# Conditioning pieces in runs, sample steps on GpSimd and rotary halves crossed by ScalarE in a hybrid decoder step

## The reference

```
mod = (silu(c) @ w_ada[l] + b_ada[l]).reshape(B, 9, D)        # conditioning, 1 prompt row + 8 sample rows
hh  = rmsnorm(x, g_pre) * (1 + m_scale) + m_shift             # before every sub-layer, per sequence
x   = x + 0.5 * m_gate * rmsnorm(f, g_post)                   # after it
proj = hh @ w_in_even                                         # layer 1: q k qi ki v wi | rq rk (4 heads) rv rg
rope(x): cat(x1*cos - x2*sin, x2*cos + x1*sin)                # rq, rk: halves of 64 of each head's 128 columns
```

## Time and profile before

| | |
|---|---|
| runs | 1423.23 us median of 3 (1422.56 to 1423.35) |
| profiled execution | 1422.14 us; its span on the core 1420.5 us |
| granted TensorE clock, mean over the span | 0.990 of full speed |
| busy in the span | PE 1357.0 us (96%), DVE 789.7 (56%), ACT 613.5 (43%), POOL 87.5 (6%) |
| pieces from POOL's queue | 96 loads of 512 KB, 4.8 us to landing (median) |

### The profile page before, as it was taken

How to read it: one execution, slowest core, us unless ns; L and a number is a source line. 1 busy time by engine, 2 the same in 40 slices (tenths; PEclk the granted TensorE clock), 3 DMA queues, 4 the chain that set the end, 5 groups by cost and what they waited for, 6 DMA issues and landing times.

```text
span 1420.5 us, 24392 instructions
## 1 busy us (share of the span) xinstructions
PE 1357.0 (96%) x9798; PEld 1256.7 (88%) x9798; DVE 789.7 (56%) x1446; ACT 613.5 (43%) x1043; POOL 87.5 (6%) x139
## 2 busy tenths in 40 slices
PE   5899999999999998999999899999989999999996
PEld 2799999979886697999999799999978888999996
DVE  1544444576697777444445743445567976444444
ACT  2534333444343455334344533334457755333342
POOL 0000000003001101000000100000011100000000
PEclk9799999999999999999999999999999999999998
DMA  9565655456249755564355556444466643444442
GB/s 364 209 210 197 205 178 187 147 199 227 90 160 341 258 210 208 180 205 151 120 163 163 206 179 207 163 135 138 159 242 224 224 163 106 148 148 150 129 150 83
DMA packets 82260, 260.08 MB, mean 183 GB/s; under 512 B 11634, under 2 KB 22962, under 8 KB 82034
## 3 DMA queue, kind: packets, MB, share of 16 engines
q1 hardware_dynamic: 65682, 199.56, 41.9%
q0 software_dynamic: 16480, 59.15, 12.0%
HBM read 254.45 MB, written 4.23 MB: 182 GB/s over the span
## 4 chain that ended last, share of the span: by engine, by line
PE 82%; DVE 10%; DMA 3%; ACT 3%; issue 2%; SPq 1%; DVEq 0%; ACTq 0%
PE ps L1614 25%; PE ps L1615 25%; PE ps L1616 25%; PE ps L1679 3%; DMA lent_lo<-in_ada 1%; DVE w_lo L2077 1%; DVE f L2159 1%; DVE x L2145 1%; DVE f L2165 1%; DVE f L2141 1%; DVE xn_lo L2153 1%; DMA x<-in_x 1%; PE ps L589 1%; DMA a_raw<-in_ada 1%; PE ps L1701 1%
## 5 line engine op out<-in xcount | busy, mean ns | idle before, releaser
L1614 PE MATMUL ps<-xn_hi,w_hi 128*128 128x320 f32 x1808 | 573.6, 317 | 21.6 <-DVE xn_lo L2153 18.2
L1616 PE MATMUL ps<-xn_hi,w_lo 128*128 128x320 f32 x1808 | 560.9, 310 | 0.0
L1615 PE MATMUL ps<-xn_lo,w_hi 128*128 128x320 f32 x1808 | 560.8, 310 | 0.0
L2077 DVE TENSOR_TENSOR w_lo<-w_raw,w_hi 128x1024 fp32r<-128x1024 f32 (+1 forms) x357 | 382.3, 1108 | 128.3 <-ACT w_hi L1884 127.7
L1614 PEld LDWEIGHTS ps<-xn_hi,w_hi 128*128 128x128 f32 x1808 | 341.4, 189 | 50.6 <-issue 29.6
L1884 ACT ACTIVATE w_hi<-w_raw 128x1024 fp32r<-128x1024 f32 x362 | 331.6, 961 | 88.8 <-PE ps L1616 78.3
L1615 PEld LDWEIGHTS ps<-xn_lo,w_hi 128*128 128x128 f32 x1808 | 341.7, 189 | 1.4
L1616 PEld LDWEIGHTS ps<-xn_hi,w_lo 128*128 128x128 f32 x1808 | 341.5, 189 | 0.0
L1614 PE MATMUL ps<-mid_hi,w_hi 128*128 128x320 f32 x704 | 218.3, 310 | 0.3 <-DVE w_lo L2077 0.3
L1616 PE MATMUL ps<-mid_hi,w_lo 128*128 128x320 f32 x704 | 217.3, 309 | 0.0
L1615 PE MATMUL ps<-mid_lo,w_hi 128*128 128x320 f32 x704 | 217.3, 309 | 0.0
(11 more groups left out here) (282 smaller groups left out, 962.1 us busy)
## 6 DMA issues: line engine op xcount, KB each, us to landing
w_raw<-in_gu SPq DMA_DIRECT2D x176, 512.0 KB, 4.5
a_raw<-in_ada POOLq DMA_DIRECT2D x96, 512.0 KB, 4.8
w_raw<-in_down SPq DMA_DIRECT2D x64, 512.0 KB, 3.6
w_raw<-in_pj SPq DMA_DIRECT2D x58, 512.0 KB, 5.1
w_raw<-in_down SPq DMA_DIRECT2D x64, 192.0 KB, 3.6
a_raw<-in_ada SPq DMA_DIRECT2D x16, 512.0 KB, 7.1
w_raw<-in_ada SPq DMA_DIRECT2D x16, 512.0 KB, 6.6
lent_hi<-in_ada SPq DMA_DIRECT2D x8, 512.0 KB, 10.8
```

The costliest lines, as they stand in the source:

```text
L1614: pe.matmul(out, hi, xhi, start=start, stop=False)
L1615: pe.matmul(out, hi, xlo, start=False, stop=False)
L1616: return pe.matmul(out, w_lo[s][:, w_at:w_at + P], xhi, start=False, stop=stop)
L2077: dve.tensor_tensor(w_lo[s][:, cols], w_raw[:, s, cols], w_hi[s][:, cols].bitcast(F32), ALU.subtract).then_inc(w_split, 1)
```

## The change

Four things. (1) `ADA_PLAN`: pieces that were multiplied one at a time between tiles come in runs: gate0 at tiles 3, 7, 11, 15, 19 (4 each; before, one at each of tiles 2 to 21), down0 at block 1 (4; before, one at blocks 0 to 3), gate1 and gate2 at tiles 8 and 13 (4 each; before, one at tiles 6 to 13), odd tail behind blocks 5, 10 and 13 (4, 4, 5; before, one behind each of 4 to 15, two behind 5). Three transposes come one place earlier. (2) At the five boundaries the two sample steps of chunks 2 to 7 go to POOL (`samples`), chunk by chunk, after its loads for the boundary. (3) DVE's order there becomes `late_chunks`, with no pairs. (4) For blocks 10 to 17 PE's permutation is gone: ACT copies each half of the block from PSUM to the other half's partitions of `rope_b`, then the block to `proj`; the sign is in the sin table.

```diff
-ADA_PLAN += [("gate0", c, 1 if c > 1 else 0) for c in range(FC)]
-ADA_PLAN += [("down0", m, 1 if m < 4 else 0) for m in range(KC)]
+ADA_PLAN += [("gate0", c, 4) for c in (3, 7, 11, 15, 19)] + [("down0", 1, 4)]
...
-ADA_PLAN += [("gate1", c, 1 if 6 <= c < 14 else 0) for c in range(FC)]
+ADA_PLAN += [("gate1", c, 4) for c in (8, 13)]
...
-ADA_PLAN += [("gate2", c, 1 if 6 <= c < 14 else 0) for c in range(FC)]
+ADA_PLAN += [("gate2", c, 4) for c in (8, 13)]
...
-ADA_PLAN += [("odd_tail", q, 2 if q == 5 else 1) for q in range(4, 2 * KC)] + [("odd_out", ("first", 2), 3)]
+ADA_PLAN += [("odd_tail", 5, 4), ("odd_tail", 10, 4), ("odd_tail", 13, 5)] + [("odd_out", ("first", 2), 3)]
...
-ADA_TURNS = {("front", 1): [0], ("front", 2): [1], ("gate0", 9): [2], ("gate0", 17): [3], ("down0", 3): [4],
+ADA_TURNS = {("front", 1): [0], ("front", 2): [1], ("gate0", 8): [2], ("gate0", 16): [3], ("down0", 2): [4],
...
             ada_load(gp, pieces[A_SLOTS:KC])
+            for k in range(2, KC):
+                samples(gp, stage, k)
+
+        def samples(gp, stage, k):
+
+            sub = PNORM[stage]
+            fs = tokens(f[:, k, PTOK:TOK])
+            gp.wait_ge(xr_ready, 8 * sub + k + 1)
+            gp.tensor_tensor(fs, fs, per_sample(modT[:, scale_at(sub, k), 1:NCOND]), ALU.mult).then_inc(scaled_s, 1)
+            gp.wait_ge(scaled_s, (KC - 2) * (sub - 1) + k - 1)
+            gp.tensor_tensor(fs, fs, per_sample(modT[:, shift_at(sub, k), 1:NCOND]), ALU.add).then_inc(xmod_ready, 1)
...
                 if b <= 9:
-                    rotate(b - 2, b - 2, 0)
-                elif B_RQK < b <= B_RQK + 8:
-                    rotate(b - 1, b - 1 - (B_RQK - 8), 1)
+                    rotate(b - 2, b - 2)
...
+                    if B_RQK <= b < B_RQK + 8:
+                        act.wait_ge(rope_done, CR + b + h - 3)
+                        for to, of in ((0, HD), (HD, 0)):
+                            last = act.activation(rope_b[to:to + HD, h, :], ps[of:of + HD, 2 * j + h, 0:TOK], kinds[h][0],
+                                                  scale=kinds[h][1])
+                        last.then_inc(crossed, 1)
                     act.activation(proj[:, b + h, :], ps[:, 2 * j + h, 0:TOK], kinds[h][0], scale=kinds[h][1])\
...
+            def rotate_halves(b, par):
+
+                dve.wait_ge(p_evac, PB + b + 1)
+                src = proj[:, b, :]
+                dve.wait_ge(crossed, b - B_RQK + 1)
+                steps.did(dve.tensor_tensor(rope_b[:, par, :], rope_b[:, par, :], ropet[:, 3, :], ALU.mult))
+                steps.did(dve.tensor_tensor(src, src, ropet[:, 2, :], ALU.mult))
+                steps.wait()
+                dve.tensor_tensor(src, src, rope_b[:, par, :], ALU.add).then_inc(rope_done, 1)
...
+                def late_chunks():
+
+                    residual(2)
+                    scaled(2)
+                    low(1)
+                    residual(3)
+                    scaled(3)
+                    low(2)
+                    dve.wait_ge(w_split, CR + 2 * W_BASE[prep] + 3)
+                    ahead(prep, (1,))
+                    residual(4)
+                    scaled(4)
+                    low(3)
+                    for k in range(5, KC):
+                        grown(k)
+                        residual(k)
+                        scaled(k)
+                        low(k - 1)
+                    low(KC - 1)
```

More of the change, by code:

```diff
@@ L293, in build @@
         proj = pb("proj", [P, EVEN_BLOCKS, TOK])
-        perm = pb("perm", [P, 2, P])
+        perm = pb("perm", [P, P])
         cached = pb("cached", [P, NB, 3, PAST])
@@ L381, in build @@
         xr_ready = sem("xr_ready")
-        xmod_ready = sem("xmod_ready")
+        xmod_ready, scaled_s = sem("xmod_ready"), sem("scaled_s")
         xn_high = sem("xn_high")
@@ L454, in build @@
         p_evac = sem("p_evac")
-        rope_mm = sem("rope_mm")
+        rope_mm, crossed = sem("rope_mm"), sem("crossed")
         rope_done = sem("rope_done")
@@ L566, in even_constants @@
             sp_.wait_ge(moments_done, SUB["down0"] + 1)
-            sp_.dma_start(perm[:, :, :], t["perm"]).then_inc(perm_in, 16)
+            sp_.dma_start(perm[:, :], t["perm"]).then_inc(perm_in, 16)
             sp_.dma_start(ones_h[:, :], t["ones_h"]).then_inc(perm_in, 16)
@@ L583, in pe_even, with rotate @@
             base = W_BASE["even_in"]
-            def rotate(b, r, kind):
+            def rotate(b, r):
                 pe.wait_ge(p_evac, PB + b + 1)
                 pe.wait_ge(rope_done, CR + r - 1)
-                pe.matmul(ps[:, 4 + r % 2, 0:TOK], perm[:, kind, :], proj[:, b, :], start=True, stop=True)\
+                pe.matmul(ps[:, 4 + r % 2, 0:TOK], perm[:, :], proj[:, b, :], start=True, stop=True)\
                   .then_inc(rope_mm, 1)
@@ L672, in pe_even @@
             pe.wait_ge(row_ready, 6)
-            rotate(0, 0, 0)
-            rotate(1, 1, 0)
+            rotate(0, 0)
+            rotate(1, 1)
             for b in range(4, EVEN_BLOCKS):
@@ L1034, in dve_even @@
                 if B_RQK <= b < B_RQK + 8:
-                    rotate(b, b - B_RQK + 8, 0, 1)
-                    rotate(b + 1, b - B_RQK + 9, 1, 1)
+                    rotate_halves(b, 0)
+                    rotate_halves(b + 1, 1)
                 if b == 12:
@@ L2208, in normed @@
                 low(0)
-                residual(2, 3)
+                if sub:
+                    late_chunks()
+                    return
                 low(1)
-                if not sub:
-                    ahead(prep, (0,))
+                ahead(prep, (0,))
                 pair(2)
                 low(2)
-                if sub:
-                    dve.wait_ge(w_split, CR + 2 * W_BASE[prep] + 3)
                 ahead(prep, (1,))
                 low(3)
-                grown(5)
-                residual(4, 5)
                 pair(4)
-                grown(6, 7)
                 low(4)
                 low(5)
-                residual(6, 7)
                 pair(6)
@@ L2460, in tables @@
            "sel4": np.kron(np.eye(4), np.eye(32, NCOND))}
-    perm = np.zeros((P, 2, P))
+    perm = np.zeros((P, P))
     rope = np.zeros((P, 4, TOK))
@@ L2470, in tables @@
             for i in range(half):
-                perm[s + half + i, kind, s + i] = -1.0
-                perm[s + i, kind, s + half + i] = 1.0
+                if kind == 0:
+                    perm[s + half + i, s + i], perm[s + i, s + half + i] = -1.0, 1.0
             for o in (s, s + half):
                 rope[o:o + half, 2 * kind] = np.cos(ang)
-                rope[o:o + half, 2 * kind + 1] = np.sin(ang)
+                rope[o:o + half, 2 * kind + 1] = np.sin(ang) * (-1.0 if kind and o == s else 1.0)
     out["perm"], out["rope"] = perm, rope
```

## The result

The changed kernel takes 1396.82 us (median of 4 runs, 1396.23 to 1400.96) against 1423.2 before (1422.56 to 1423.35): ratio 0.9822, 95% interval 0.9802 to 0.9841. Two repetitions gave 1397.83 and 1397.49, each beside the kernel before, which had 1422.07 and 1422.92 there. So the gain is 24.2, 25.4 and 26.4 us in three sets.

The account below looks back on a forecast made before the run. PE was taken as the bound, with 82% of the chain that ended last. Savings of 9.5 + 1.2 + 4.3 + 7.3 = 22.3 us off 1422.14 gave 1399.8, or 1400.9 us for the median; range 1397.5 to 1406.

Parts of the forecast that it names:

- Pieces in runs: Gate and down stages: 28 places fewer at 0.32 us and two beside transposes at 0.25 save 9.5 us.
- Odd tail: Odd tail: twelve places become three; the ACT and DVE chain behind block 9 lets 1.2 us through, bounds 0.3 to 2.2.
- Rotation: even_in: eight PE permutations of 0.54 us go, ACT's extra copies are covered, 4.3 us saved.
- Boundaries: Five boundaries: PE's stops at chunks 4 and 6 go, 1.75 us at four and 0.33 before gate3, 7.3 in all.
- 1.2 to spare: Boundaries: estimated slack in us between low(7) done, 11.3 after scaled(2) starts, and PE beginning chunk 7 at 12.5.
- Loads at nothing: Loads of pieces, in runs and at boundaries, were expected in time and costed at nothing.
- low end: Fast end of the range, 1397.5 us: odd tail 2.2, rotation 4.5, and 2 us more if attention starts sooner.
- rival (b): Loads come late: the odd tail's first run and one or two others stand 2 us each, 1405 us; chance 0.07.
- Rival (c): DVE bounds even_in, or the odd chain takes nothing: rotation gives 2.5, odd tail 0.3, 1403.6 us; chance 0.10.
- Rival (a): Boundaries: POOL and DVE block each other, 1412.4 us in full, 1404 by half; chance 0.17, mostly the half.
- longer than 0.49: Sign that the forecast is wrong: DVE's residual and low in the boundaries grow longer than 0.49 us.
- Rival (d): Boundaries, chunks 2 to 7: POOL's operation has a long fixed cost T, PE stands 12 T - 11.1; slower, chance 0.03.

Follow-up runs that it names:

- the late tail: Changed kernel with gate0's and down0's pieces in runs of six and the odd tail's behind blocks 10, 13, 15 (5, 5, 3): 1398.09 us.
- the order without GpSimd: Kernel before with only VectorE's new chunk order at the boundaries, sample steps kept on VectorE: 1423.49 us against 1422.07.
- loads first: Changed kernel with runs of six in gate0 and down0, and GpSimd issuing each boundary's last two loads before its w_lo half: 1414.03 us.

## Why the prediction was right, and where it was not

- **Pieces in runs, 9.5: right.** 9.33 alone, 9.2 without the spread of gate0's start.
- **Odd tail, 1.2: right**, 1.04, inside its bounds. Of its reasons, "0.87 us for two pieces fewer" and ACT coming late both show; "The chain starts behind block 9" gave PE nothing more, as the late tail showed.
- **Rotation, 4.3: right**, 4.32.
- **Boundaries, 7.3: the step that failed.** "So PE runs dry at chunks 4 and 6: 1.35 + 0.50 us" took the brackets for the price; start to start it is 2.36, at five boundaries 11.8. The pieces came out right because they were priced start to start. The second half of the miss is gate3: "Before gate3 PE stands at 1173.30 for the load of a piece ... which the change doesn't touch", so only 0.33 was counted. That wait had been hidden behind DVE's; 2.37 was won there (249.61 to 247.24). "4 x 1.75 + 0.33" should have been 5 x 2.36. The picture of the state after was wrong as well, and it was luck that this cost little: "at 1.7 us per chunk, below PE's 1.76" is 1.85, "no later than ACT's step" is 0.3 us later, and the slack of "1.2 to spare" is 0.3 at chunk 7 and none at chunks 4 to 6 where no load is late. `low(7)` ends 12.37 us after `scaled(2)` starts (11.3 forecast), and PE takes chunk 7 at 12.66 (12.5 forecast).
- **Loads at nothing: wrong in small.** They take back 1.7 to 2.6 us before gate1, gate2 and odd_in by the columns, against waits of 1.0 to 2.6 (the third execution has 0.45 more of waiting for `ra` in odd_in). That is rival (b), at the boundaries and not at the runs, where no run waited.
- **The sum.** 9.33 + 1.04 + 4.32 + 11.8 = 26.5; less 1.7 to 2.6 for the loads that now count, 23.9 to 24.8. Attention was 1.1 to 2.3 us shorter than in before's profile, as in kernels where only other stages were changed, so that is spread and no gain of the change. The medians differ by 24.2 to 26.4, and the second and third profile from before's by 24.6 and 25.0. That the first median lies below the low end is thus the mis-sized boundaries and up to 2 us of this spread; which part is which was not shown. Rival (c) did not come in; the low end had 2 us for an attention that starts sooner, where the column of attention shows only its usual spread. The medians of the four parts alone add up to 29.3, their segments to 25.7.
- **Rival (a), half at 1404: no.** Residuals beside GpSimd went from 482 to 496 ns on average (0.59 us once a boundary, 0.49 at most else), `low` stayed at 487; GpSimd bore the rest (448 and 340 ns against 0.30 alone). The sign "longer than 0.49" came in and was named too tightly: it is 0.1 us a boundary. "By that rule the time is one of these two" did not follow, since operations this short meet for a part of their length. The block itself is real.
- **Rival (d):** T is 0.30 us alone, as taken, and 0.39 on average. Its formula, PE standing 12 T - 11.1, is refuted: with four operations a chunk, as long as T = 0.75 would be, it gives nothing, and 1.6 us a boundary were lost.

## What to carry to other kernels

Price a wait from the start of the last instruction before it to the start of the second one after it, less the steps that would pass anyway; the wait in brackets left out a sixth of the cost here at the long stop and a third to near half at the short ones. When a stall goes, ask which hidden waits stood beside it, here loads of 0.2 to 1.3 us, and look at the spacing of the consumer's starts, not only at its listed waits: 1.85 us against 1.76 showed that VectorE still led. In this kernel two small operations a chunk on GpSimd were cheap, with 0.27 us to spare, and four were not; one long operation there has to be kept off VectorE's critical chain; and a run of filler work did best where the engine would wait.

## What was not expected

- One GpSimd operation of 2.37 us held one of VectorE's residuals up by 2.38 us, the whole of it, though twelve short ones at a boundary lengthen residuals by 14 ns on average.
- The clock of TensorE fell from 2.4 to 1.2 GHz in some executions: at 1139 in one of three profiles of the same kernel (granted 0.55, 2.5 us), at the same place (1162) in the order without GpSimd (0.51, 2.6 us), and behind the 3.58 us wait with loads first (0.51 of full speed).
- Order and engine of the boundary change gain -0.2 and 1.0 us each, and 2.37 together.
